# Two weight loads ahead of two expert loads, and a second buffer with a new order at the start of the even layer

## What is computed

```python
# first block: end of the mixer, then the experts
o = _rms(o) * norm_w * silu(z)
h = o.reshape(bsz, seq, GDN_VAL_WIDTH) @ w_out          # 2048 -> 1024
x = _layernorm(ALPHA * x + h, g, b)
h = _hier_moe(x, ...)                                   # 32 experts, 3 matrices each
...
# second block: start of the even layer
xn = rmsnorm(x, g_norm)
q, k, v, o, z_a, gates, u, z_b = _split(xn @ w_in, EVEN_SPLITS)
qk = silu(causal_conv(concatenate([q, k]), conv_w))     # 4 taps along the tokens, per channel
```

## Time and profile before

| | us |
|---|---|
| median of 3 runs | 1015.89 |
| lowest, highest | 1015.7, 1017.44 |
| the profiled execution, its own time | 1013.74 |
| its span, first to last instruction | 1012.4 |
| TensorE busy in it | 968.9 |
| VectorE busy | 548.3 |
| ScalarE busy | 329.3 |

### The profile page before, as it was taken

How to read it: one execution, slowest core, us unless ns; L and a number is a source line. 1 busy time by engine, 2 the same in 40 slices (tenths; PEclk the granted TensorE clock), 3 DMA queues, 4 the chain that set the end, 5 groups by cost and what they waited for, 6 DMA issues and landing times.

```text
span 1012.4 us, 21876 instructions
## 1 busy us (share of the span) xinstructions
PE 968.9 (96%) x9305; PEld 757.2 (75%) x9305; DVE 548.3 (54%) x1160; ACT 329.3 (33%) x872; POOL 52.5 (5%) x81
## 2 busy tenths in 40 slices
PE   9999999999999999799867899999999999999999
PEld 6888888888888894345323588988888988877887
DVE  3875866866868334111100596875555465184675
ACT  3455456446536222001100223132121331233550
POOL 1111011011000000000000000000000000024000
PEclk9999999999999999899987999999999999999999
DMA  8213214234146998999999934442555344552221
GB/s 345 88 64 134 99 65 157 76 110 180 70 150 262 423 399 353 428 430 429 434 430 410 411 157 148 169 172 84 180 187 174 140 167 167 187 189 83 84 84 42
DMA packets 33622, 211.61 MB, mean 209 GB/s; under 512 B 4385, under 2 KB 8929, under 8 KB 15089
## 3 DMA queue, kind: packets, MB, share of 16 engines
q1 hardware_dynamic: 33520, 210.16, 53.8%
HBM read 209.03 MB, written 1.11 MB: 208 GB/s over the span
## 4 chain that ended last, share of the span: by engine, by line
PE 82%; DMA 7%; SPq 5%; DVE 3%; ACT 2%; issue 2%; POOL 0%; ACTq 0%; DVEq 0%; POOLq 0%
PE ps L552 11%; PE ps L3138 9%; PE ps L578 5%; PE ps L3038 5%; SPq L1888 4%; DMA xt<-in_wu 4%; PE ps L3809 3%; PE ps L2002 3%; PE ps L3778 3%; PE ps L3907 2%; PE ps L2647 2%; PE ps L794 2%; PE ps L958 2%; PE ps L3178 2%; PE ps L2884 2%; PE ps L600 2%
## 5 line engine op out<-in xcount | busy, mean ns | idle before, releaser
L552 PE MATMUL ps<-xt,slots 128*128 128x256 f32 x512 | 122.3, 384 | 0.0
L552 PEld LDWEIGHTS ps<-xt,slots 128*128 128x128 f32 x512 | 93.8, 190 | 12.8 <-issue 0.4
L1288 DVE SCALAR_TENSOR_TENSOR arena<-arena 128x256 f32<-128x256 f32 x128 | 56.1, 496 | 0.0
L2002 PE MATMUL ps<-arena 128*32 128x512 f32 x224 | 47.7, 635 | 6.9 <-DMA arena<-in_w 6.1
L2342 DVE TENSOR_TENSOR arena<-arena,ps 128x256 f32<-128x256 f32 x8 | 3.4, 421 | 88.8 <-ACT arena L2132 88.8
L2002 PE MATMUL ps<-slots,arena 128*32 128x512 f32 x192 | 47.5, 640 | 2.5 <-DMA xt<-in_wu 2.5
L4310 POOL TENSOR_TENSOR arena<-arena 128x512 f32<-128x512 f32 (+1 forms) x8 | 17.8, 2260 | 596.5 <-DVE arena L4118 596.5
L2132 ACT ACTIVATE arena<-ps 128x256 f32<-128x256 f32 x8 | 3.1, 385 | 114.2 <-PE ps L2002 114.2
L2002 PEld LDWEIGHTS ps<-arena 128*32 128x32 f32 x224 | 11.8, 115 | 26.7 <-issue 19.6
L3809 PE MATMUL ps<-xt,slots 128*128 128x256 f32 x128 | 30.6, 385 | 0.6 <-ACT arena L4010 0.6
L958 PE MATMUL ps<-slots,yt 128*128 128x256 f32 x128 | 28.6, 380 | 2.0 <-DMA slots<-in_wu 2.0
(11 more groups left out here) (584 smaller groups left out, 2115.9 us busy)
## 6 DMA issues: line engine op xcount, KB each, us to landing
slots<-in_wu SPq DMA_DIRECT2D x91, 1024.0 KB, 5.9
arena<-in_wu SPq DMA_DIRECT2D x20, 1024.0 KB, 14.4
arena<-in_w SPq DMA_DIRECT2D x5, 4096.0 KB, 28.9
slots<-in_w SPq DMA_DIRECT2D x8, 2048.0 KB, 34.0
extra<-in_w SPq DMA_DIRECT2D x2, 4096.0 KB, 29.4
yt<-in_w SPq DMA_DIRECT2D x3, 2048.0 KB, 30.5
extra<-in_wu SPq DMA_DIRECT2D x4, 1024.0 KB, 19.5
xt<-in_wu SPq DMA_DIRECT2D x4, 1024.0 KB, 30.7
```

Source lines behind the costliest of these rows:

```text
L552: q = M.matmul(bank(b, T), self.slots[:, s, k, n * P:(n + 1) * P], self.xt[:, k, :], start=(k == 0), stop=(k == KT - 1))
L1288: q = V.scalar_tensor_tensor(g.cn[:, s], src, w, g.cn[:, s], ALU.mult, ALU.add)
L2002: q = M.matmul(self.ps[r, 2, :], g.xg[:, half * (KT // 2) + k, r], self.flat(slots[e])[:, k * 512:(k + 1) * 512], start=(half == 0 and k = ...
```

## The change

1. In `gdn_sync` the fills of slots 3 and 2 (column groups 2 and 3 of the output's second half) stand ahead of the wait and the fills of expert slots 9 and 8, where they stood behind them.
2. In `embed_scalar` the squares of the first two column pieces stand one before each of the last two gates, ahead of the table load, where they stood behind it.
3. `raw` gets a twin for the second half of the rows (`raws[1]`), laid over memory that the layer uses only later. The waits for the convolution fall away, and the clearing of the zero columns is done for both.
4. TensorE does the piece `chunk(1, 2)` ahead of the product with the diagonal. VectorE makes the diagonal ahead of `mix_qk(0, 3)`.
5. VectorE's order of convolutions: `convolve(0)` and half of `convolve(1)` go right behind `raw_rows`, ahead of the mixing for the second pair; the rest of `convolve(1)` and `convolve(2)` go where 0 and 1 were; `convolve(3)` alone is left ahead of the third pair's folds; `convolve(6)` goes ahead of the forget gates.

```diff
@@ gdn_sync
         self.fill(0, U_GOUT + 1)
         self.fill(1, U_GOUT + 3)
+        self.fill(3, U_GOUT + 5)
+        self.fill(2, U_GOUT + 7)
         SP.wait_ge(*g.u_scaled(QKH))
         for u in (8, 9):
             self.fill(RING[u], U_MOE + u)
-        self.fill(3, U_GOUT + 5)
-        self.fill(2, U_GOUT + 7)
         self.fill(RING[10], U_MOE + 10)
@@ embed_scalar
         gate(2, "21", late)
         keep(1)
+        square(0)
         gate(3, "22", slice(1, 2))
+        square(1)
         gate(3, "12", slice(0, 1))
         A.preload_act_table_set("natural_log_exp_and_others")
-        square(0)
-        square(1)
         keep(2)
@@ even
+        raw_at = self.top
         g.ww = (al("w0", [P, AH, P]), al("w1", [P, AH, T]))
...
+        g.raws = (g.raw, self.arena[:, raw_at:raw_at + 8 * (T + 3)].rearrange("p (a b) -> p a b", a=8))
@@ even_tensor
         self.chunk(0, 2)
+        self.chunk(1, 2)
         M.wait_ge(*g.diag_made(1))
         for t in range(NT):
             q = M.matmul(bank(5, P, t * P), c["ones"], g.diag[:, t], start=True, stop=True, skip_group_check=True)
         q.then_inc(*g.r_spread.up())
-        for s, k in ((1, 2), (0, 3), (1, 3)):
-            self.chunk(s, k)
+        for s in range(2):
+            self.chunk(s, 3)
@@ even_scalar
             if j == 0:
-                A.wait_ge(*g.raw_clear(1))
-            else:
-                A.wait_ge(*g.convolved(4 * j))
+                A.wait_ge(*g.raw_clear(2))
             row = 2 * g.qk_slots[j][0]
-            A.activation(g.raw[:, row:row + 2, 3:3 + P], first.rearrange("p (n t) -> p n t", n=2), ACT.Copy).then_inc(
+            A.activation(g.raws[(j + 1) // 2][:, row:row + 2, 3:3 + P], first.rearrange("p (n t) -> p n t", n=2), ACT.Copy).then_inc(
@@ even_vector
-            low, high = (g.raw[:, 2 * s:2 * s + 2, 3:3 + T] for s in g.qk_slots[j])
+            low, high = (g.raws[(j + 1) // 2][:, 2 * s:2 * s + 2, 3:3 + T] for s in g.qk_slots[j])
...
-                if j > 0:
-                    V.wait_ge(*g.convolved(4 * j))
...
-                    o, src = g.qk[:, j, :], g.raw[:, row, tap:tap + T]
+                    o, src = g.qk[:, j, :], g.raws[u // 4][:, row, tap:tap + T]
...
-        V.memset(g.raw[:, :, 0:3], 0.0).then_inc(*g.raw_clear.up())
+        for raw in g.raws:
+            V.memset(raw[:, :, 0:3], 0.0).then_inc(*g.raw_clear.up())
         mix_qk(0, 1)
         mix_qk(0, 2)
...
-        mix_qk(0, 3)
         V.wait_ge(*g.st_exp(1))
         for t in range(NT):
             q = V.tensor_scalar(g.diag[:, t], c["ident"], r[:, t:t + 1], None, ALU.mult)
         q.then_inc(*g.diag_made.up())
+        mix_qk(0, 3)
         mix_qk(0, 4)
...
         raw_rows(0)
         raw_rows(1)
+        convolve(0)
+        convolve(1, (0, 1))
         mix_qk(1, 1)
         mix_qk(1, 2)
...
         fold_qk(0, 4)
-        convolve(0)
-        convolve(1)
+        convolve(1, (2, 3))
+        convolve(2)
         for n in range(3):
             fold_qk(1, n)
...
-        convolve(2)
         convolve(3)
         for n in range(5):
             fold_qk(2, n)
-        convolve(4)
-        convolve(5)
+        for u in (4, 5, 6):
+            convolve(u)
         V.wait_ge(*g.gates_kept(1))
...
-        convolve(6)
         convolve(7)
```

More of the change, by code:

```diff
@@ L3402, in even_vector @@
         q.then_inc(*g.diag_made.up())
+        mix_qk(0, 3)
         mix_qk(0, 4)
-        V.wait_ge(*g.raw_clear(1))
+        V.wait_ge(*g.raw_clear(2))
         V.wait_ge(*g.loaded(4))
```

## The result

| | us | against before |
|---|---|---|
| before, median of 6 | 1015.9 (1014.53 to 1018.29) | |
| changed, median of 6 | 1020.36 (1019.74 to 1022.6) | ratio 1.004, 95% interval 1.0025 to 1.0056 |
| profiled execution, changed | 1019.74, span 1018.4 | before 1013.74, span 1012.4 |

What follows compares the result with a forecast made beforehand. TensorE, on 82% of the chain, was taken as the bound: time is won only where it stands still or its DMA stream moves. Terms -0.1 + 0.45 = +0.35 us gave 1016.2 us against 1015.89, range 1013.0 to 1018.3.

Steps and rivals of the forecast that it cites:

- What would show it: Signs: line 958 without wait, 1.5 to 2.3 us at line 1928, DMA dent near 334.5, one even-layer gap near 2 us.
- Part 2: Even layer: moved squares, projection piece and convolutions lengthen one TensorE gap by 0.8 us and remove 0.34: net +0.45 us.
- Part 1: GDN output: moving two fills ahead of two expert fills removes a 2.04 us wait, but only 0.1 us arrives: -0.1.
- third gap: Even layer, TensorE's 0.34 us wait before 656.68 for VectorE's folds; forecast to go, -0.34 us.
- first gap of 1.95: Even layer, TensorE's wait before the first pair's sixth product, forecast to grow from 0.62 to 1.95 us.
- Only part 1 is won: Rival: the GDN output gives -2.04 us, the even layer costs +0.45: -1.6 us, 1014.3 us; chance 0.15.
- both waits are really won: Rival: GDN output gives 2.04 us and even layer 1.49: -3.5 us, 1012.4 us; chance 0.15.
- the backlog: GDN output: routing inputs queue behind earlier DMA transfers, 14.1 us to land, so issuing them 2 us sooner gives nothing.
- hole: GDN output: DMA queue runs dry near 334.3 before the new fill flows; taken as 0.4 us, bounds 0 to 0.8.
- The hole is wide: Rival: queue dry for 2 us, TensorE 1.4 us later at line 1928, with part 2 +1.9, 1017.8 us; chance 0.10.
- The table loads: Rival, even layer: moved squares between sigmoids need four table loads, 5.1 us; TensorE 4.3 us late, 1020.5 us; chance 0.05.

Runs made afterwards that it cites:

- part-1 kernel: Kernel before with only the fills of slots 3 and 2 moved ahead of the expert fills in `gdn_sync`, even layer unchanged: 1020.82 us, ratio 1.0045.
- part 2 alone: Kernel before with all of the change except `gdn_sync`, so the fills stay as before: 1016.23 us, ratio 1.0003.
- the run with one expert transfer ahead: Part-1 kernel, but the fill of expert slot 9 stays ahead of the two moved fills and only slot 8's goes behind: 1018.17 us, ratio 1.0018.
- the mended kernel: Changed kernel with the last column group ahead of the route-weight wait and the first pair's first two folds ahead of the second pair's mixing: 1011.76 us, ratio 0.9953.
- part 1 with the group first: Part-1 kernel with TensorE's last column group of the second token half ahead of the wait for the route weights: 1014.11 us, ratio 0.9978.

## Why the prediction was wrong

**Where the waits go: right.** The signs named under "What would show it" came: line 958 without a wait, 1.5 to 2.3 us at line 1928 behind the routing inputs (2.54 here), a dent near 334.5 (311 GB/s against 434, though not in the DMA share), no gap at the diagonal, one near 2 us before the first pair's sixth product (1.88), none before the third pair's.

**Their sizes: right in sum, in part by luck.** Part 2 was sized at +0.45, and its true delays were -0.79 + 1.25 - 0.58 = -0.12, mainly because a removed stop gives back some 0.25 us more than its idle time. Part 1 was sized at -0.1 and moved line 1928 by +0.43. The last routing input was issued 1.74 us sooner than before, took 17.2 us to land instead of 14.1, and so VectorE's folding began at 364.38 instead of 363.05; less the 0.52 us of this execution that is 0.8 us later, and I had taken 0.4. Both delays together are 0.31 us against the +0.35 forecast: two errors of about half a microsecond, which cancel.

**The step that failed** is the premise at the start of the prediction, on which the sum was built: that a microsecond is won only where TensorE stands still or where its DMA stream moves, taken to mean that a standstill costs its own length. I moved a stop of 2.04 us to line 1928 and let 0.3 us of the third gap pay for a first gap of 1.95, and priced each by where TensorE resumed. No term of the sum and no rival said what the products behind a stop cost, so that cost stood at nothing without a reason. In the changed kernel's profile they ran at half the granted clock for about 6.9 us behind line 1928, which cost 3.41 us, and again in the even layer, which cost 1.63. The part-1 kernel (+4.6 us), its filling by four useless products (+1.15) and by two (+5.3) show that the first of these makes nearly all of the loss in the medians, and that it hangs on how long TensorE stands idle and what fills that time. The second shows only in profiles, as part 2 alone lost nothing in its median. The prediction had the old stop of 2.04 us at line 958 before it, which shows no half clock behind it, and that is what misled: the clock may hold at one place and fall at another, and may hold or fall in two executions of one kernel. Why it holds or falls in a given execution stays open.

**The rivals.** "Only part 1 is won" and "both waits are really won" were rightly held unlikely because of the backlog: the run with one expert transfer ahead has no hole, and still no gain. "The hole is wide": the hole exists, and delays the folding by 0.8 us in the changed kernel's profile and by 1.4 in part 1's, not by 2. The table loads did not come: there is one load, behind the moved squares. That the measured 1020.36 us lie next to that rival's 1020.5 is chance. The page "ScalarE: Activation LUTs" of the Trainium skill, section "Table sets: the hidden batching unit", does not name the square among the cheap functions that are in every set; in this case's trace the squares run between sigmoids without a load.

**What to look for next time** was in reach. The Trainium skill, page "TensorE: Matmul & The Clock Gate", section "Part 1: The HAM clock gate", has the array's clock at one of two levels, 1.2 or 2.4 GHz. The windows agree, 0.50 and 1.00. By these two levels a fall costs up to half of the time at the lower one. An estimate for the 6.9 us at half clock between 366 and 374 is 3.4 us, and 3.41 were measured. Whether the clock would fall at the new place, no row of the kernel before tells.

## What to carry to other kernels

Before you remove a wait, find the wait that takes its place. It may be longer or worse placed, and what stands behind it may run slower: look behind each stop for the granted clock, not only at its length. When a hidden transfer is what is late next, put real work of the same engine ahead of its wait (here the order of two blocks turned +4.6 us into -2.1). Judge such a change by the scatter of many executions, as one profile shows one draw.

## What the runs showed that was not expected

- Unused products made a kernel faster: 3.4 us less (+1.15 us against +4.6, each against its own "before") for 1.7 us more work on the engine that bounds it.
- Behind the same stop of 1.88 us the clock fell in the changed kernel's profile and held in part 2's; it held once behind a stop of 3.08 us, and fell behind one of 1.65 us.
- A stop that goes gave back about 0.25 us more than the idle time that the timeline shows for it.
- The clock fell without any stop in the profiled execution of the mended kernel, during the narrow products between 373 and 379 us. From line 1928 to line 1973 it took 14.02 us against 11.23 in part 1 with the group first, which has the same order of work there, so about 2.8 us were lost, mostly at line 1945 (x26 in 5.84 us against 3.15). This was its slowest execution, 1013.97. So a standstill is not the only thing that the clock can fall behind:

```profile
370.00:374.00 4.00, 3.96 (x31) 3.74 (x31) 1.78 (x6) 2.71 (x7) 0.00 (x0) 0.83 1.01 428
374.00:378.00 4.00, 4.00 (x20) 4.00 (x20) 2.66 (x18) 1.27 (x4) 0.00 (x0) 0.50 1.02 420
```
